# Three edits to the order of work in a transformer kernel: the recurrence's exponentials, the mixer projection's start, the MLP's first down tiles

## The reference, cut to what matters

```python
# both layers of the first block
y = jnp.square(jax.nn.relu(h @ w_up[i])) @ w_down[i]          # 1024 -> 4096 -> 1024
...
# second block: 8 heads of 128, decays from bcum = cumsum(log f)
o = o + jnp.einsum('bhtk,bhkv->bhtv', qt * jnp.exp(bcum), state)
state = (jnp.exp(blast[:, :, 0, :])[..., None] * state
         + jnp.einsum('bhsk,bhsv->bhkv', kt * jnp.exp(blast - bcum), vt))
...
o = rms_norm_2(o, hg_norm_g[l].reshape(HG_HEADS, HG_DV)).reshape(B, S, HG_VW)
y_a = (o * jax.nn.silu(zg)) @ w_a[l]                          # the mixer projection
merged = jax.nn.sigmoid(zga) * y_a + jax.nn.sigmoid(zgb) * y_b
h = h + g1 * (merged @ w_out[l])
```

## Time and profile before

| | |
|---|---|
| median of the three runs | 3690.22 us (3679.05 to 3694.79) |
| the profiled execution's own time | 3677.86 us |
| span of its instructions | 3676.1 us |
| busy: TensorE, VectorE, GpSimd, ScalarE | 89%, 61%, 54%, 21% of the span |
| chain that ended last: TensorE, DMA, VectorE | 63%, 19%, 12% of the span |
| mean granted TensorE clock | 0.959 of full speed |
| HBM traffic | 735 MB read, 8 MB written |

### The profile page before, as it was taken

One profiled execution on the slowest core, in us unless ns is written; L12 is line 12 of the kernel. 1 busy time (PEld: TensorE's weight loads), 2 busy tenths in 40 slices (PEclk: granted clock), 3 DMA queues, 4 the chain that ended last, 5 costly groups with the idle time before them and its releaser, 6 DMA issues.

```text
span 3676.1 us, 34982 instructions
## 1 busy us (share of the span) xinstructions
PE 3254.6 (89%) x12579; PEld 2186.6 (59%) x12579; DVE 2245.8 (61%) x4215; ACT 755.2 (21%) x1502; POOL 1978.7 (54%) x1214
## 2 busy tenths in 40 slices
PE   8999989998978899989999889989988777877776
PEld 6778878886845688868877667644433333333332
DVE  4756543336544433358925667767777877777775
ACT  3462331112036311120112331201001111101000
POOL 2453259886400598859867448234444444444442
PEclk8999999999979999999999989999999999999999
DMA  4350023222410132223432202699999999999997
GB/s 130 126 180 4 1 69 103 92 92 80 160 47 1 58 103 92 93 90 95 140 98 80 81 21 95 258 410 410 412 412 414 422 421 422 420 420 418 405 421 321
DMA packets 272554, 745.78 MB, mean 203 GB/s; under 512 B 13065, under 2 KB 198930, under 8 KB 206866
## 3 DMA queue, kind: packets, MB, share of 16 engines
q0 software_dynamic: 73728, 536.90, 35.4%
q1 hardware_dynamic: 194464, 200.34, 17.3%
q10 hardware_dynamic: 4210, 6.56, 0.5%
HBM read 735.37 MB, written 8.39 MB: 202 GB/s over the span
## 4 chain that ended last, share of the span: by engine, by line
PE 63%; DMA 19%; DVE 12%; issue 3%; ACT 3%; POOL 1%; ACTq 0%; DVEq 0%; POOLq 0%
DMA arena<-in_peer_uv,rstd 16%; PE bank L1209 12%; PE bank L1210 12%; PE bank L1211 12%; PE bank L1681 9%; PE bank L1597 1%; PE bank L1615 1%; PE bank L1696 1%; DVE arena L3039 1%; PE bank L1491 1%; PE bank L1396 1%; DMA weight_ring<-in_peer_uv,rstd 1%; DMA normed<-in_peer_uv,rstd 1%; PE bank L1127 1%; PE bank L1413 1%
## 5 line engine op out<-in xcount | busy, mean ns | idle before, releaser
L1073 POOL DMA_INDIRECT arena<-in_peer_uv,rstd x419 | 469.9, 1121 | 655.1 <-PE bank L1681 603.7
L1211 PE MATMUL bank<-split_arena 128*128 128x512 f32 x1776 | 697.6, 393 | 0.0
L1008 POOL TENSOR_TENSOR split_arena<-weight_ring,ones 128x1024 fp32r<-128x1024 f32 x218 | 537.1, 2464 | 271.9 <-PE bank L1211 211.0
L3039 DVE CUSTOM_DVE_ANT_0 arena<-arena,branch 128x1024 f32<-128x1024 f32 x419 | 512.5, 1225 | 261.6 <-DMA arena<-in_peer_uv,rstd 259.2
L1209 PE MATMUL bank<-split_arena 128*128 128x512 f32 x1392 | 551.6, 396 | 27.7 <-DVE split_arena L2427 19.3
L1010 POOL TENSOR_TENSOR split_arena<-weight_ring,split_arena 128x1024 fp32r<-128x1024 f32 x218 | 556.5, 2553 | 17.1
L1210 PE MATMUL bank<-split_arena 128*128 128x512 f32 x1392 | 545.2, 392 | 0.0
L1681 PE MATMUL bank<-arena,level_mask 128*128 128x512 f32 x840 | 410.4, 632 | 117.6 <-DVE level_mask L3020 117.6
L1681 PE MATMUL bank<-arena,row_diagonals 128*128 128x512 f32 x836 | 388.4, 606 | 65.3 <-DVE row_diagonals L3020 65.1
L1211 PEld LDWEIGHTS bank<-split_arena 128*128 128x128 f32 x1776 | 335.7, 189 | 74.1
L1681 PEld LDWEIGHTS bank<-arena,level_mask 128*128 128x128 f32 x840 | 162.6, 201 | 344.8 <-DVE level_mask L3020 170.3
(11 more groups left out here) (450 smaller groups left out, 4960.8 us busy)
## 6 DMA issues: line engine op xcount, KB each, us to landing
weight_ring<-in_w_up SPq DMA_DIRECT2D x32, 1024.0 KB, 5.4
weight_ring<-in_w_down SPq DMA_DIRECT2D x32, 1024.0 KB, 5.1
weight_ring<-in_w_in SPq DMA_DIRECT2D x32, 1024.0 KB, 5.8
weight_ring<-in_ada_w SPq DMA_DIRECT2D x24, 1024.0 KB, 5.3
weight_ring<-in_w_in_a SPq DMA_DIRECT2D x13, 1024.0 KB, 7.7
weight_ring<-in_w_out SPq DMA_DIRECT2D x12, 1024.0 KB, 7.5
weight_ring<-in_w_in_b SPq DMA_DIRECT2D x10, 1024.0 KB, 7.7
weight_ring<-in_peer_wq SPq DMA_DIRECT2D x10, 1024.0 KB, 25.8
```

What stands on the lines that cost most here:

```text
L1008: pool.tensor_tensor(hi, part, bc_mid(ones[:], DT), ALU.mult).then_inc(split_hi, 1)
L1073: pool.indirect_dma_start(row_slots[slot_of[r]], None, a["peer_uv"], bass.IndirectOffsetOnAxis(ap=experts[n % 2][:, c:c + 1], axis=0)).the ...
L1211: return pe.matmul(psum[t.bank][:], hi, a_lo[k], start=False, stop=last)
L3039: dve.tensor_tensor_reduce(row, row, h_tok[:, r // NE, :], 1.0, 0.0, ALU.mult, ALU.add, dots[:, i % 4, j:j + 1]).then_inc(dot_ready, 1)
```

## The change

Four places change; no operation is added or taken away.

1. ScalarE, recurrence: the copy of the former head's output out of bank 7 moves behind the exponentials of `h_kdec` and `h_eb`.
2. GpSimd, behind head 7: the first half of the mixer projection's weights is split when all the pairs of the last head are done (`h_pairs` at 56), no longer when `h_tail` has reached 4. The second half still waits for `h_tail` at 8.
3. TensorE, behind head 7: the first two tiles of the mixer projection are begun between the last steps of the recurrence: tile 0 with k 0 to 4 ahead of `hgrn_out(7)`, tile 1 with k 0 to 2 behind it, tile 1 with k 3 and 4 behind `head_sum(7)`, then both with k 5 to 7.
4. TensorE, MLP: the first two down tiles of each quarter run side by side over k.

```diff
--- block.gpsimd
-                place = ((h_tail, HH // 2 * (i + 1)) if i < 2 else (bank_out[t.bank], t.use) if i < 4 else
+                place = ((h_pairs, HH * LEVELS) if i == 0 else (h_tail, HH) if i == 1 else (bank_out[t.bank], t.use) if i < 4 else
--- block.tensor: split_first
-            def split_first(us, w, tiles, a_hi, a_lo, ready, order=range(DT)):
+            def split_first(us, w, tiles, a_hi, a_lo, ready, order=range(DT), part=slice(0, DT)):
-                for i, k in enumerate(order):
+                for i, k in list(enumerate(order))[part]:
                     ready(i)
                     for j, t in enumerate(tiles):
+                        if t is None:
+                            continue
--- block.tensor: mlp
-                    for j, u in enumerate(m["units"]):
...
-                            def ready(k):
-                                if j == 4 and h == 0:
-                                    pe.wait_ge(up_ready, i * QT + (FT * l + k + 1))
-
-                            split_product(u, h, mlp_w, t, each(a_hi), each(a_lo), ready)
+                    def begin(u, h, t):
+                        pe.wait_ge(split_ready, i * 16 + u.split + h + 1)
+                        pe.wait_ge(bank_out[t.bank], i * 2 + (t.use - 1))
+
+                    for n in range(first, 8):
+                        u, h, t = m["units"][n // 2], n % 2, m["up_tiles"][n]
+                        begin(u, h, t)
+                        split_product(u, h, mlp_w, t, each(in_hi), each(in_lo))
+                    u = m["units"][4]
+                    for k in range(DT):
+                        pe.wait_ge(up_ready, i * QT + (FT * l + k + 1))
+                        for h, t in enumerate(m["down_tiles"][0:2]):
+                            if k == 0:
+                                begin(u, h, t)
+                            x = split_steps(u.split + h, mlp_w, t, each(hid_hi), each(hid_lo), k, k == 0, k == DT - 1)
+                            if k == DT - 1:
+                                x.then_inc(half_done, 1)
+                    for n in range(2, 8):
+                        u, h, t = m["units"][4 + n // 2], n % 2, m["down_tiles"][n]
+                        begin(u, h, t)
+                        split_product(u, h, mlp_w, t, each(hid_hi), each(hid_lo))
--- block.tensor: behind the heads
+            def mixer_first(tiles, part):
+
+                split_first(ya_units, out_w, tiles, each(split_H), each(mixed_lo),
+                            lambda k: pe.wait_ge(in_split, IN_MIXED + k + 1), part=part)
+
             hgrn_kv(HH - 1)
             head_sum(HH - 2)
+            mixer_first(ya_tiles[0:1], slice(0, HH - 3))
             hgrn_out(HH - 1)
+            mixer_first([None, ya_tiles[1]], slice(0, HH - 5))
             head_sum(HH - 1)
+            mixer_first([None, ya_tiles[1]], slice(HH - 5, HH - 3))
+            mixer_first(ya_tiles[0:2], slice(HH - 3, HH))
--- block.scalar: the heads
-                if h:
-                    take(hg[h - 1]["o"], hq_f[:, h - 1, :])
                 act.wait_ge(h_sub, (h + 1) * (LEVELS + 1))
                 act.activation(h_kdec, h_kdec, ACT.Exp)
                 if h:
                     have(act, hg[h - 1]["kv"])
                 act.activation(h_eb, hb_f[:, h, :], ACT.Exp).then_inc(h_tail, 1)
                 if h:
+                    take(hg[h - 1]["o"], hq_f[:, h - 1, :])
                     full(act, hg[h - 1]["kv"])
```

14 lines of the change are left out of this document (3 added, 11 removed).

## The result

| | kernel before | changed kernel |
|---|---|---|
| median of the runs taken side by side | 3687.20 us (3679.05 to 3694.79, 4 runs) | 3649.05 us (3637.55 to 3650.70, 4 runs) |
| the profiled execution | 3677.86 us | 3648.11 us |
| span | 3676.1 us | 3646.4 us |
| mean granted clock | 0.959 | 0.964 |

The ratio is 0.989, with a 95% interval of 0.986 to 0.9921. The forecast was 3651.6 us, within 3637 to 3672, and "faster by over 0.5%" came true. Run again later, beside other kernels, the change took 3646.53 us against 3677.76, a ratio of 0.9912 (0.9898 to 0.9925).

A forecast was written before the change was run, and what follows sets the result against it. TensorE, busy 89% of the span, was taken as the bound, with DMA bounding the gathering. Gains 14.7 + 7.1 + 8.3 + 8.5 = 38.6 us took the median from 3690.2 to 3651.6 us, range 3637 to 3672.

The forecast's parts named there:

- Edit 1 in the heads: Heads 1 to 6: earlier exponentials remove TensorE's 2.45 us wait per head, 14.7 us; steadier clock adds 7.1 us.
- the falls: Heads: drops of TensorE's clock to 1.2 GHz behind the idle 2.45 us, taken as gone for 7.1 us.
- Rival 1: Heads and new wait before k 6: the clock falls anyway; gain 27.5 us, 3663 us; chance 0.13.
- Rival 2: Heads: exponentials stay late behind something unseen, so wait and clock falls remain; 3677.5 us; chance 0.05.
- The tail: Head 7 to the end of the projection's first pair: 7.8 + 0 + 2.0 - 1.5 = 8.3 us gained.
- Edit 2 puts the split behind the pairs ... Gain 7.8: Head 7: from the pairs' start, TensorE's transpose starts after 6.2 us instead of 14.1, gaining 7.8 us.
- Edit 3: Mixer projection's early start: little yield, a 5.7 us wait before k 6, and half clock behind it losing 1.5 us.
- Edit 4: MLP: side-by-side down tiles remove six stalls on VectorE's last low part, gaining 8.5 us.
- Six stalls: 6 x 1.42: MLP quarters 1 to 3, both MLPs: six stalls of 1.42 us each go, together 8.5 us.
- TensorE wants it at 21.8: MLP down weights: GpSimd has half 4 split 16.1 us into the pair, before TensorE needs it at 21.8.
- Rival 3: Tail: the moved split holds all five VectorE operations behind the pairs; gain 30.3 us, 3660 us; chance 0.11.
- Rival 4: MLP: GpSimd's splitting sets the pace, 5.9 us per half against TensorE's 5.44; slower, 3719 us; chance 0.03.

The follow-up runs named there:

- Edit 1 alone: Kernel before with only ScalarE's copy moved behind the exponentials; 3652.08 us against 3684.28, ratio 0.9913.
- the two matmuls in front of the wait: Kernel before, copy not moved, plus two idle-time matmuls before the wait for the decayed key in heads 1 to 6; 3670.76 us against 3682.54, ratio 0.9974.
- edits 1 and 4 alone: Kernel before with only ScalarE's copy moved and the MLP's down tiles side by side; 3638.82 us against 3677.76, ratio 0.9898.
- the two kernels without edits 2 and 3: Kernel before with ScalarE's copy moved, without and with the MLP's down tiles side by side; ratios 0.9913 and 0.9898.
- edit 4 alone: Kernel before with only the MLP's down tiles side by side; 3672.03 us against 3684.28, ratio 0.9958.

## Why the prediction was right, and which steps were not

**Edit 1 in the heads: right.** Forecast 14.7 and 7.1 us, of which 21.7 ahead of head 6's product; measured 22.8, with a scatter of some 3 us from the falls. The wait was worth 2.67 us a head instead of 2.45. The value's transpose waits for the copy, but only 0.25 us. Edit 1 alone gives all of it, and the two matmuls in front of the wait show that the falls were its consequence, as the forecast took them. Rival 1 (they come anyway) fails in the heads. Rival 2 (the wait is only renamed) fails altogether.

**The tail: right in size and nearly so in each step, wrong in what it was credited to.** Forecast 8.3 us (8.4 from head 6's product), measured 7.4. From the start of level 6's pairs to the transpose the forecast had 6.2 us and the profile has 6.4 (2164.48 to 2170.84); on to `hgrn_out(7)` it had 8.1 and has 8.1 (2178.91); on to `mix(7)` it had 6.2 and has 6.2. The step that failed is "Edit 2 puts the split behind the pairs ... Gain 7.8". It booked under edit 2 what is for the most part edit 1's: with edits 1 and 4 alone, the pairs still held, the way from the pairs to the transpose takes 8.6 us (2159.44 to 2168.01), against 14.1 before. VectorE no longer stands 5.38 us for late exponentials. Over the whole stretch to the gather the two kernels without edits 2 and 3 gain 7.8 and 10.1 us, and the change 7.4. Edit 2 takes the 4.2 us from the pairs, and the next operations pay them. The sum counted the held product in their place ("the product ends 0.5 us behind them"), but behind it three held operations "in both kernels", where the rows have two in each (2869 and 2808 before, 2886 and 2825 in the change). It never asked what edit 1 does there by itself, which only the runs showed.

**Edit 3: the yield and its price were named rightly, the price too low.** The wait before k 6 was forecast as 5.7 us and measured as 6.07, the last six matmuls, k 7's, at half clock as 2.6 us and measured as 2.73. The loss from `mix(7)` on was forecast as 1.5 us ("a little more behind them" included) and measured as 2.7: 0.4 up to k 7 and 2.3 behind it. What was missing is VectorE's share, the later first tile and one more meeting with a split.

**Edit 4: right in mechanism, off in size.** Forecast 8.5 us, measured 6.2. The mis-sized term is "Six stalls: 6 x 1.42". All six are gone, but the first quarter, which had no stall to lose, gained a wait of 0.6 us in each MLP (0.7 to 0.8 us in all). I had asked only about half 4 of the down weights ("TensorE wants it at 21.8") and not about the second one, which the pair wants 4.8 us earlier than before. The rest is at the MLPs' ends, where the norm waits longer for VectorE's last addition. The 0.6 us were named in the text as what would be wrong: a new wait of the down tiles on GpSimd.

**Rivals 3 and 4.** Rival 3 is nearest in mechanism at the tail, with three of the five operations held, and its claim that "edits 2 and 3 yield nothing at the tail" is what the runs of edits 1 and 4 alone show. Its price of 8.3 us was wrong, since edit 1 pays that; and with edit 3 in place, edit 2 did yield 2.9 us in the profile. Rival 4 is out: GpSimd had 4.99 us to spare in a quarter.

**The total.** Forecast 38.6 us. Up to the first gather the profile gains 36.8: the MLP lacks 2.3 us and the tail 1.0, the heads give 1.1 more, and 0.4 us come from stages that nothing touched. The medians differ by 38.2 us here and by 31.2 in the repetition, whose interval (0.9898 to 0.9925) ends just short of the forecast's ratio, 1 - 38.6/3690.2 = 0.9895. So the fit of the first medians is closer than the terms deserve, and in part luck.

## What to carry to other kernels

Where several edits meet in one stretch, work out what each does there alone before you book a gain under one of them: here the edit in the heads had taken the tail's gain already. Moving an operation of GpSimd away from two of VectorE's only moves the hold to the next two; what helped was a place where VectorE had nothing of that kind to do, behind its last low part. And work that is begun early pays only if what it runs up against is early too.

## What the runs showed of the hardware

The alternation of the two engines is carried on. In the projections one GpSimd operation and one held operation of VectorE follow each other for some 45 us, and the difference between 2.67 and 0.94 us in its first member stands beside 2.3 us at its end. In between, the two-input operation that reads one operand from PSUM (2911) takes 0.69 us, so it is not held; in head 7 COPY_PREDICATED (2882) takes 0.72 to 0.74 us beside a split too. The Trainium skill (SBUF — State Buffer, Who interferes with whom) says the same: outside its 2-port modes, a VectorE instruction with at most one input in SBUF doesn't contend with GpSimd. The trace agrees with 0.69 us against 2.7 to 2.9.

The granted clock can differ between executions of the same instructions: 0.92 and 1.00 in the same stretch behind head 6's product with edit 1 made and edits 2 and 3 not. In the heads as they were before, the five periods from head 1's product to head 6's were 22.55, 25.01, 22.57, 25.10 and 23.63 us in one profile and 25.39, 23.63, 25.02, 22.55 and 25.12 in that of edit 4 alone. The mean over a stretch hides where the half clock ends: with 0.76 over the same 14 us, k 7's matmuls took 2.73 us in one kernel and 1.60 in another. In the heads, two matmuls that cut an idle time of 2.45 us to 0.73 removed every fall to 1.2 GHz.
